# Three places of a two-block transformer kernel: where the spatial weights are scaled, how the last convolution tile of a third is taken, and where the last square sums stand at the gate exit

## What is computed

```
def spatial_gating(z_uv, sgu_norm, w_spatial, b_spatial):   # 8 heads of 128, chunks of 128 tokens
    z = gelu(z_uv); u, v = z[..., :1024], z[..., 1024:]
    v = rmsnorm(v, sgu_norm)
    mixed = einsum('hts,bnshd->bnthd', w_spatial * tril, v) + b_spatial
    return u * mixed

def conv_ffn(h, w_up, conv_w, conv_b, w_down):              # D_FF = 2816, causal width 3
    conv = conv_b + sum_k conv_w[k] * shifted(h @ w_up, k)
    a, b = conv[..., :D_FF], conv[..., D_FF:]
    return (gelu(a) * b) @ w_down
...
gate = sigmoid(rmsnorm(x, ple_norm) @ w_ple_gate)           # the gate exit
x = x + gate * (p @ w_ple)
x = rmsnorm(x, final_norm)                                  # then the second block: rmsnorm, swiglu, ...
```

## Time and profile before

| | us |
|---|---|
| median of 3 runs (2710.96 to 2715.09) | 2711.43 |
| the profiled execution | 2712.36 |
| its span, first to last instruction | 2711.1 |
| PE busy in it | 2664.5 (98%) |
| DVE, ACT, POOL busy | 1433.2, 975.8, 322.4 |
| mean granted TensorE clock | 0.994 |

### The profile page before, as it was taken

One profiled execution on the slowest core, in us unless ns is written; L12 is line 12 of the kernel. 1 busy time (PEld: TensorE's weight loads), 2 busy tenths in 40 slices (PEclk: granted clock), 3 DMA queues, 4 the chain that ended last, 5 costly groups with the idle time before them and its releaser, 6 DMA issues.

```text
span 2711.1 us, 31399 instructions
## 1 busy us (share of the span) xinstructions
PE 2664.5 (98%) x12844; PEld 2228.9 (82%) x12844; DVE 1433.2 (53%) x2234; ACT 975.8 (36%) x1612; POOL 322.4 (12%) x391
## 2 busy tenths in 40 slices
PE   9999999999999999998999999999999989999999
PEld 8897888788787788888888888888888788888887
DVE  7536547564657444356675443544434577543433
ACT  4343334342454222245553222322222576422221
POOL 0000010000021000024530000100000587300000
PEclk9999999999999999999999999999999999999999
DMA  5321225523232445463332232323232100233231
GB/s 158 125 94 63 98 89 168 170 78 109 70 102 94 105 101 105 99 103 95 98 89 94 93 103 95 97 94 109 88 99 73 55 32 32 94 103 100 94 94 61
DMA packets 280935, 258.93 MB, mean 96 GB/s; under 512 B 40261, under 2 KB 275800, under 8 KB 280792
## 3 DMA queue, kind: packets, MB, share of 16 engines
q1 hardware_dynamic: 280775, 256.93, 31.8%
q10 hardware_dynamic: 16, 0.00, 0.0%
HBM read 242.23 MB, written 14.68 MB: 95 GB/s over the span
## 4 chain that ended last, share of the span: by engine, by line
PE 87%; DVE 7%; ACT 4%; issue 1%; POOL 1%; ACTq 0%; POOLq 0%; DVEq 0%
PE bank L1124 28%; PE bank L1126 28%; PE bank L1125 28%; DVE Wl L1824 2%; PE bank L1282 1%; ACT Wh L1476 1%; DVE TMP L2032 1%; DVE TMP L2029 1%; ACT TMP L1598 1%; PE bank L1135 0%; PE bank L1335 0%; DVE Pl L1812 0%; DVE bank L1891 0%; DVE TMP L2038 0%; DVE Pl L2304 0%
## 5 line engine op out<-in xcount | busy, mean ns | idle before, releaser
L1124 PE MATMUL bank<-Hh,Wl 128*128 128x512 f32 x2144 | 842.2, 393 | 3.8 <-DVE Hl L1843 3.8
L1126 PE MATMUL bank<-Hh,Wh 128*128 128x512 f32 x2144 | 835.6, 390 | 0.0
L1125 PE MATMUL bank<-Hl,Wh 128*128 128x512 f32 x2144 | 835.4, 390 | 0.0
L1824 DVE TENSOR_TENSOR Wl<-RAW,Wh 128x1024 fp32r<-128x1024 f32 (+2 forms) x420 | 492.9, 1217 | 160.3 <-ACT Wh L1476 159.6
L1476 ACT ACTIVATE Wh<-RAW 128x1024 fp32r<-128x1024 f32 (+2 forms) x454 | 441.0, 1022 | 370.7 <-PE bank L1126 336.7
L1124 PEld LDWEIGHTS bank<-Hh,Wl 128*128 128x128 f32 x2144 | 402.7, 188 | 91.0 <-issue 4.8
L1124 PE MATMUL bank<-Ph,Wl 128*128 128x512 f32 x1200 | 471.8, 393 | 5.2 <-DVE Pl L1812 4.9
L1125 PEld LDWEIGHTS bank<-Hl,Wh 128*128 128x128 f32 x2144 | 402.9, 188 | 85.2 <-issue 1.7
L1126 PEld LDWEIGHTS bank<-Hh,Wh 128*128 128x128 f32 x2144 | 402.5, 188 | 85.1
L1126 PE MATMUL bank<-Ph,Wh 128*128 128x512 f32 x1200 | 467.9, 390 | 0.0
L1125 PE MATMUL bank<-Pl,Wh 128*128 128x512 f32 x1200 | 467.5, 390 | 0.0
(11 more groups left out here) (308 smaller groups left out, 2415.8 us busy)
## 6 DMA issues: line engine op xcount, KB each, us to landing
RAW<-in_ffn_wg SPq DMA_DIRECT2D x44, 1024.0 KB, 5.3
RAW<-in_ffn_wu SPq DMA_DIRECT2D x44, 1024.0 KB, 5.3
RAW<-in_ffn_wd SPq DMA_DIRECT2D x32, 1024.0 KB, 5.1
RAW<-in_w_up SPq DMA_DIRECT2D x22, 1024.0 KB, 5.1
RAW<-in_w_in SPq DMA_DIRECT2D x20, 1024.0 KB, 5.2
RAW<-in_ffn_wd SPq DMA_DIRECT2D x16, 768.0 KB, 4.4
bias_scratch<-M SPq DMA_DIRECT2D x16, 512.0 KB, 8.1
RAW<-in_w_down SPq DMA_DIRECT2D x8, 1024.0 KB, 6.5
```

Of the source, the lines that this page charges most:

```text
L1124: mm(o, ll, rh, start=start, stop=False)
L1125: mm(o, lh, rl, start=False, stop=False)
L1126: return mm(o, lh, rh, start=False, stop=stop)
L1824: tt(Wl[:, n % 3, x:y], RAW[:, n % 2, x:y], f(Wh[:, n % 3, x:y]), ALU.subtract).then_inc(*w_lo.up(*([("w_lo", n)] if i else [])))
```

## The change

There are three edits to the order of steps, and the splitting of two steps into two each that it needs.

1. Mixing: `ws_pair` loses its scaling, which becomes a step `ws_raw`; `mix` loses its pair, which becomes `mix_pair`. Per head the order was mix(h-1) with its pair, scaling(h), pair of WS(h); it is scaling(h), mix(h-1), pair of WS(h), pair of mix(h-1).
2. Convolution network: in the last j of each third, the `b` tile is taken output by output: product, scale, convolution, product and pair of output 0 stand in the list before product and scale of output 1. The order of PE's own work is the same.
3. Gate exit: the sums of chunks 5, 6 and 7 stand behind the eighth `h_pair`; they stood behind gate_x(5), behind the third `h_pair`, and at the end.

```diff
-                else:
-                    nb = next_tile(tag + "b", (h, j), 1 if kind == "conv" and j == n // 2 - 1 else 2)
-                    dense(bb, nb, 8, "H", scaled=True)
-                    do("used", nb)
+                apart = kind == "conv" and j == n // 2 - 1
+                if not begins:
+                    nb = next_tile(tag + "b", (h, j), 1 if apart else 2)
+                    if not apart:
+                        dense(bb, nb, 8, "H", scaled=True)
+                        do("used", nb)
                 for c in range(2):
                     t = ("t_a", tag, h, j, c)
+                    if apart:
+                        dense([bb[c]], nb, 8, "H", kw=c, scaled=True)
+                        if c:
+                            do("used", nb)
...
-    def ws_pair(h):
+    def ws_raw(h):
         tmps.take(("t_ws", h))
-        do("ws_pair", h)
+        do("ws_raw", h)
     def mix(h):
         banks.take(("b_mix", h))
         tmps.take(("t_mix", h))
+        do("mix", h)
+
+    def mix_pair(h):
         pv[8 + h] += 1
-        do("mix", h, pv[8 + h])
+        do("mix_pair", h, pv[8 + h])
...
             if h:
+                ws_raw(h)
                 mix(h - 1)
-                ws_pair(h)
+                do("ws_pair", h)
+                mix_pair(h - 1)
...
         for c in range(2):
             gate_x(2 * i + c)
-            sums_x(2 * i + c)
+            if 2 * i + c < 5:
+                sums_x(2 * i + c)
...
-    for c in range(3):
+    for c in range(4):
         h_pair(c, None)
-    sums_x(6)
-    h_pair(3, None)
     scale([("pg", 3, 1)])
     for c in (4, 5):
         h_pair(c, None)
     gate_x(7)
     for c in (6, 7):
         h_pair(c, None)
-    sums_x(7)
+    for c in (5, 6, 7):
+        sums_x(c)
```

More of the change, by code:

```diff
@@ L520, in mix @@
         tmps.take(("t_mix", h))
+        do("mix", h)
+    def mix_pair(h):
         pv[8 + h] += 1
-        do("mix", h, pv[8 + h])
-    ws_pair(0)
+        do("mix_pair", h, pv[8 + h])
+    ws_raw(0)
+    do("ws_pair", 0)
     for i in range(4):
@@ L538, in order @@
     mix(7)
+    mix_pair(7)
     tmps.join(utmps)
@@ L1260, in pe_program @@
             elif kind == "mix":
-                h, _ = s
+                h, = s
                 o = vacant(("b_mix", h))
@@ L1564, in act_program @@
                 h, = s
-                act.wait_ge(*at(("ws_scaled", h)))
+                act.wait_ge(*at(("ws_raw", h)))
                 if h:
@@ L1568, in act_program @@
                 run(WS[:, 0, :], tmp(("t_ws", h)), ACT.Copy).then_inc(*pair_hi.up(("ws_hi", h)))
-            elif kind == "mix":
+            elif kind == "mix_pair":
                 h, ver = s
@@ L1955, in dve_program @@
                         *dve_out.up(("ws_T", half), free=("b_ws", half)))
-            elif kind == "ws_pair":
+            elif kind == "ws_raw":
                 h, = s
@@ L1962, in dve_program @@
                     ins = ts(t[:, 128 * q:128 * q + 128], wsp[:, h, :], rv[:, q:q + 1], None, ALU.mult)
-                ins.then_inc(*dve_out.up(("ws_scaled", h)))
+                ins.then_inc(*dve_out.up(("ws_raw", h)))
+            elif kind == "ws_pair":
+                h, = s
                 dve.wait_ge(*at(("ws_hi", h)))
-                tt(WS[:, 1, :], t, f(WS[:, 0, :]), ALU.subtract).then_inc(*pair_lo.up(("ws", h), free=("t_ws", h)))
+                tt(WS[:, 1, :], tmp(("t_ws", h)), f(WS[:, 0, :]), ALU.subtract).then_inc(*pair_lo.up(("ws", h), free=("t_ws", h)))
             elif kind == "mix":
-                h, ver = s
+                h, = s
                 m = vacant(("t_mix", h))
@@ L1975, in dve_program @@
                 tt(m, m, tmp(("t_u", h)), ALU.mult).then_inc(*dve_out.up(("mixed", h), free=("t_u", h)))
-                low_of("p", 8 + h, ver, m, ("p_hi", 8 + h, ver), ("t_mix", h))
+            elif kind == "mix_pair":
+                h, ver = s
+                low_of("p", 8 + h, ver, tmp(("t_mix", h)), ("p_hi", 8 + h, ver), ("t_mix", h))
             elif kind == "neg_rows":
```

## The result

The changed kernel takes 2705.34 us (median of 9 runs, 2704.45 to 2706.69) against 2712.26 (9 runs beside it): a ratio of 0.9973, 95% interval 0.9964 to 0.9982. It is 6.9 us faster. The forecast was 2705.0 and 6.4 us. The numbers of lines changed: L1124 is now L1137, L1812 is L1825, L1843 is L1856, L1232 is L1245, L1824 is L1837.

What follows compares the result with a forecast made beforehand. PE, busy 98%, was taken as the bound, so only its idle time could be won. Mixing -5.2, thirds -2.7, gate exit 0 and clock +1.4 sum to -6.5 us; predicted 2705.0 us, range 2700.5 to 2708.8.

Steps and rivals of the forecast that it cites:

- Mixing, -5.2: Mixing of the heads: DVE's chain behind each mixing is the bound and goes, no wait on WS left: -5.2 us.
- Thirds, -2.7: Last convolution tile of each third, output by output: first +0.6, middle -0.5, last -2.8, together -2.7 us.
- Gate exit, earlier start: Gate exit: PE's wide tile starts 1.5 us earlier, at 824.3 instead of 825.79.
- Forecast of the wait: Gate exit, behind the wide tile: PE stands still 2.7 to 3.7 us for POOL's sums.
- of the one-column products: Gate exit, behind the wait for POOL's sums: earlier start given back almost whole, so 0 us taken.
- Gate exit, clock, +1.4: Behind the gate exit's new wait: PE likely left at the lower clock when dense work resumes, +1.4 us.
- The gate exit that wins: Rival, gate exit: additions end before PE asks, no clock lost, -3.6 in place of +1.4, 2700.0 us; chance 0.10.
- the thirds that win nothing: Rival, last third: second scale lands in the chain, 2.8 become a loss of 0.6, 2708.4 us; chance 0.11.
- the scaling that delays the mixing: Rival, mixing: DVE's chain stays the bound, scaling paid for seven heads, +6.1 instead of -5.2, 2716.3 us; chance 0.04.
- The gate exit that gets worse: Rival, gate exit: every POOL addition takes 1.73, +3.4 in place of +1.4, 2707.0 us; chance 0.15.

Runs made afterwards that it cites:

- experiment 1: Kernel before with the mixing edit alone, the other two edits taken back: 2706.25 us against 2711.81.
- experiment 2: Kernel before with the output by output order of the thirds alone: 2708.83 us against 2711.81.
- 8: Changed kernel with the scaling back behind bias and gelu(u) of the head before, pairs still in the new order: 2706.66 us.
- 9: Changed kernel with the scaling still ahead of the mixing, but the two pairs in the order of before: 2704.94 us.
- experiment 3: Kernel before with the gate exit edit alone: 2714.53 us against 2711.81.
- experiment 5: Changed kernel with 28 transposes of the identity on PE ahead of the wait for POOL's sums: 2702.85 us against the kernel before's 2711.77.
- 4: Changed kernel with the gate exit's order of before, so mixing and thirds together: 2704.87 us against the kernel before's 2711.81.
- 6: Changed kernel with the six additions of the sums of chunks 5 to 7 on DVE instead of POOL: 2703.42 us against the kernel before's 2711.77.
- 7: Changed kernel with the six additions on DVE and the first third in its old order: 2700.54 us against the kernel before's 2711.77.
- 11: Repeat of the changed kernel with the gate exit's order of before, in the same rounds as the changed kernel: 2705.92 us.
- 12: Repeat of the changed kernel with the six additions on DVE, in the same rounds as the changed kernel: 2700.14 us.
- experiment 10: The changed kernel itself, run once more: 2705.14 us, ratio 0.9974 to the kernel before.

## Why the prediction was right, point by point

- **Mixing, -5.2.** Measured -5.3 by place and -5.6 alone (experiment 1). That a third wait lay hidden under the slow clock is shown by the three waits in experiment 2. The working had one reading wrong: the 5.0 us of the chain run from DVE's bias, not from PE's mixing. From the mixing it is 5.1 to 5.2 without a split, which is under PE's 5.4 and bounds nothing, and 6.9 with one. The chain was the bound only together with the weight split in the same queue. The forecast came out because its 5.2 was read from PE's places and not from the chain. For the new order I had 2.4 and 4.4 us; it is 2.2 and 2.6. I had not seen that half of the edit would do (8, 9).
- **Thirds, -2.7.** By place it is +0.5, -0.9, -3.4, together -3.8 (experiment 2), where before and the run have slow clock in the same third; the medians say -3.0. All three signs and the cause of the loss in the first were right. The middle and the last were undersized by 0.4 and 0.6; the last third's norm lost its wait of 0.38 too, which I had not counted.
- **Gate exit, earlier start.** Forecast 1.5 us, measured 1.57. Forecast of the wait 2.7 to 3.7, measured 3.52; of the one-column products -0.9 to +0.1 against before, measured +0.04 (-1.57 + 1.61). The collision with the split is in the rows (2.30 and 4.03), and only at the last addition: the first five took 1.32 to 1.34.
- **Gate exit, clock, +1.4.** This is the term that was mis-sized. It measured +4.4 (3.3 in experiment 3): 1.7 in the one-column products, which I had taken to run at full clock, and 2.65 in the tile behind. I had taken the price of one window at 0.57 (1.7 us); PE was at 1.2 GHz for the whole 9 us behind the wait. That it hangs on the wait is shown by all five traces with the wait of 3.5 us, which have it, by experiment 5 in part, and by 4, 6, 7, 11 and 12, where both are gone. That the slow clock of before cost nothing there, as I had assumed, is shown by trace 11.
- **Sum.** The parts by place, the thirds from experiment 2, are -5.3 - 3.8 + 4.4 = -4.7 us, against the forecast's -6.5; the medians of the three edits alone add up to -5.8. The two profiled executions differ by 7.9 (2712.36 and 2704.45): the rest is 1.0 in a first third that had no slow clock this time, 1.9 in the attentions and 0.3 ahead of the mixing, none of it made by an edit as far as the runs show. So a total of 6.9 in the medians, beside a forecast of 6.4, is in part luck: a term too low by 3 us was met by thirds that won 1.1 more than forecast and by the clock elsewhere.
- **Rivals.** The gate exit that wins, the thirds that win nothing and the scaling that delays the mixing did not happen. The gate exit that gets worse did, by another way than the one written: the clock, and not POOL's additions at 1.73. The range ended at 2700.5, half a us short of the first rival's 2700.0.
- **Open.** What the gate exit edit is worth in company. Alone it costs 2.7 us by the median, with an interval that reaches to none; at its place it costs 3.3 to 4.6 us in every profiled run; but by the medians, with or without it, the changed kernel takes the same within 0.8 us. The two of eight runs without it that lie near 2701 (experiment 11) have a mean granted clock of 0.996 and 0.997, the six near 2706 have 0.994 or 0.995, so the spread goes with the clock. Whether it is scatter or follows from the moment at which the attention begins, I can't say from these runs.

## What to carry to other kernels

When a steady stretch of products waits every second round, count the time from the end of one round's product to the next one's operand, against PE's own pace, and count in it what only every second round puts into the same queue, here the weight split. Once enough steps are off that chain the whole loss is gone, and more buys nothing; either half of the edit did it here. The loss is read from PE's places, since waits can be hidden by a slow clock (3.1 us of waits, 5.3 lost). Taking the last outputs one at a time pays only where the engine that finishes them is idle when the first is ready; where it is late, what filled a gap for nothing lands in the chain. Work that is moved out of the way of a start needs somebody to be done by: look for its reader, and give it to the engine that the new order has left idle, here DVE instead of POOL.

## What the runs showed of the hardware

- The same POOL addition takes 1.32 to 1.34 us alone and 2.30 where DVE's split wants the same moment; DVE's split then takes 4.03 instead of 2.36. Four `Hl` take 4.79 beside POOL and 2.73 alone.
- In the changed kernel's trace a wait of 3.5 us was followed by about 9 us at 1.2 GHz, and the clock was already low when the wait ended, so that the one-column products took 3.4 us, not 1.7. The same kernel's wait of 2.7 us on `Pl` in the first third was followed by a clock of 0.61 in one execution (experiment 10, 492 to 496) and of 1.00 in the other. Waits of 1.6 us in the mixing were followed by 0.57 in before and by a full clock in experiment 2.
- With PE kept busy by 28 transposes during the wait the clock was full through the one-column products, but the four us behind them had a mean of 0.57 (experiment 5).
- A low clock cost nothing where PE waited for its operands anyway: the wide tile of the old order took 13.53 us with it and 13.55 without (before and experiment 11).
- The first attention, with the same waits, took 186.9 us in one execution and 191.0 in another of the same kernel, with a granted clock of 0.99 and 0.96. The median of five runs of one kernel was 2703.4 in one group and 2700.1 in another (experiments 6 and 12), so 2 us between two medians of this kernel prove little; places of PE within a stretch tell more.
